# Low sample columns of the normed x moved behind its high columns, in an fp32r decoder step on one core

## The reference

```
h = rmsnorm(x, norm_g) @ w_in            # 12824 columns: q, k, v, gates and z paths of three branches
o_nsa, o_moba, o_mem = three attentions
branches = (o_b * silu(z_b)) @ w_br_b    # for each of the three
y = x + sum(sigmoid(gate_logits) * branches) @ w_out
```

## Time and profile before

| | us |
|---|---|
| median of 3 runs | 1113.56 (1112.87 to 1113.68) |
| span of the profiled execution, first to last instruction | 1110.9 |
| TensorE busy | 1100.0 |
| VectorE busy | 606.3 |
| ScalarE busy | 419.5 |
| GpSimd busy | 66.8 |

### The profile page before, as it was taken

How to read it: one execution, slowest core, us unless ns; L and a number is a source line. 1 busy time by engine, 2 the same in 40 slices (tenths; PEclk the granted TensorE clock), 3 DMA queues, 4 the chain that set the end, 5 groups by cost and what they waited for, 6 DMA issues and landing times.

```text
span 1110.9 us, 19312 instructions
## 1 busy us (share of the span) xinstructions
PE 1100.0 (99%) x8020; PEld 1077.8 (97%) x8020; DVE 606.3 (55%) x884; ACT 419.5 (38%) x566; POOL 66.8 (6%) x121
## 2 busy tenths in 40 slices
PE   9999999999999999999999999999999999999996
PEld 7998999999999999999999999999999999999996
DVE  6794443536456667664454467455455454454445
ACT  6733322424335444443333344333333333333332
POOL 0014000000000000001100000000000000002220
PEclk9999999999999999999999999999999999999998
DMA  8556685544444232358888744544544444464342
GB/s 297 196 189 201 228 279 189 179 152 152 168 147 173 83 113 110 114 171 295 288 277 306 257 149 171 171 171 171 171 167 153 168 145 144 147 242 146 148 150 95
DMA packets 64081, 202.03 MB, mean 182 GB/s; under 512 B 6647, under 2 KB 35607, under 8 KB 45831
## 3 DMA queue, kind: packets, MB, share of 16 engines
q1 hardware_dynamic: 58888, 185.68, 48.8%
q0 software_dynamic: 2400, 10.89, 2.8%
q10 hardware_dynamic: 2718, 4.41, 1.1%
HBM read 193.61 MB, written 11.53 MB: 185 GB/s over the span
## 4 chain that ended last, share of the span: by engine, by line
PE 99%; DVE 1%; issue 0%; DVEq 0%
PE bank L1327 27%; PE bank L1328 27%; PE bank L1329 27%; PE bank L1679 1%; PE bank L1360 1%; PE bank L1455 1%; PE bank L1450 1%; PE bank L1429 1%; PE bank L1428 1%; PE bank L1427 1%; PE bank L1594 1%; PE bank L1517 0%; PE bank L1452 0%; PE bank L1685 0%; PE bank L1345 0%; PE bank L1454 0%
## 5 line engine op out<-in xcount | busy, mean ns | idle before, releaser
L536 ACT ACTIVATE w_hi<-raw 128x2048 fp32r<-128x2048 f32 x140 | 268.1, 1915 | 572.2 <-PE bank L1329 479.9
L1327 PE MATMUL bank<-h_hi,w_hi 128*128 128x320 f32 x1536 | 479.7, 312 | 0.0
L1329 PE MATMUL bank<-h_hi,w_lo 128*128 128x320 f32 x1536 | 474.6, 309 | 0.0
L1328 PE MATMUL bank<-h_lo,w_hi 128*128 128x320 f32 x1536 | 474.5, 309 | 0.0
L814 DVE TENSOR_TENSOR w_lo<-raw,w_hi 128x2048 fp32r<-128x2048 f32 x140 | 325.2, 2323 | 186.4 <-ACT w_hi L536 186.2
L1327 PEld LDWEIGHTS bank<-h_hi,w_hi 128*128 128x128 f32 x1536 | 288.4, 188 | 3.9 <-issue 3.5
L1328 PEld LDWEIGHTS bank<-h_lo,w_hi 128*128 128x128 f32 x1536 | 288.5, 188 | 0.4
L1329 PEld LDWEIGHTS bank<-h_hi,w_lo 128*128 128x128 f32 x1536 | 288.4, 188 | 0.0
L1328 PE MATMUL bank<-oz_lo,w_hi 128*128 128x320 f32 x256 | 78.9, 308 | 0.0
L1329 PE MATMUL bank<-oz_hi,w_lo 128*128 128x320 f32 x256 | 78.8, 308 | 0.0
L1327 PE MATMUL bank<-oz_hi,w_hi 128*128 128x320 f32 x256 | 78.8, 308 | 0.0
(11 more groups left out here) (347 smaller groups left out, 1127.5 us busy)
## 6 DMA issues: line engine op xcount, KB each, us to landing
raw<-in_stream SPq DMA_DIRECT2D x140, 1024.0 KB, 5.0
cmp_t<-in_cmp_pages SPq DMA_DIRECT2D x32, 128.0 KB, 4.2
kt_moba<-in_moba_k SPq DMA_DIRECT2D x16, 256.0 KB, 3.6
kt_mem<-in_mem_k SPq DMA_DIRECT2D x8, 512.0 KB, 6.3
vs_moba<-in_moba_v SPq DMA_DIRECT2D x16, 256.0 KB
vs_mem<-in_mem_v SPq DMA_DIRECT2D x8, 512.0 KB
out_win_old<-in_cache_win POOLq DMA_DIRECT2D x8, 512.0 KB, 3.7
raw<-in_stream SPq DMA_DIRECT2D x10, 256.0 KB, 9.9
```

The source lines that it names most:

```text
L536: nc.scalar.activation(w_hi[:, u], raw[:, u], ACT.Copy).then_inc(hi_ready[u], 1)
L1327: nc.tensor.matmul(out[:, 0:n], w_hi[:, u, kb, :], hi[:, kb, :], start=(kb == first), stop=False)
L1328: nc.tensor.matmul(out[:, 0:n], w_hi[:, u, kb, :], lo[:, kb, :], start=False, stop=False)
L1329: mm = nc.tensor.matmul(out[:, 0:n], w_lo[:, u, kb, :], hi[:, kb, :], start=False, stop=(kb == last))
```

## The change

The storage of h_hi and h_lo (320 + 320 columns a block) is cut anew: `h_wide` has 384 columns a block, the 320 high ones and behind them the 64 low ones of the samples; `h_low` has the 256 low ones of the prompt. With w_hi, a block multiplies h_wide's 384 columns into columns 0 to 384 of the bank, and h_low's 256 into columns 0 to 256; with w_lo, h_wide's first 320. The low part of the samples so ends up in columns 320 to 384 of the bank, and VectorE adds it: it scales it into a spare of 64 columns, scales the 320, and adds the spare to the last 64. The number of matmuls and the total of moving columns of a block (960) stay.

```
+WIDE = TOK + N_SMP
-        h_hi = fixed("h_hi", [P, KB, TOK], f32r)
-        h_lo = fixed("h_lo", [P, KB, TOK], f32r)
+        h_wide = fixed("h_wide", [P, KB, WIDE], f32r)
+        h_low = fixed("h_low", [P, KB, SEQ], f32r)
+        h_hi = h_wide[:, :, 0:TOK]
...
+            def low_columns(kb):
+                dve.wait_ge(hi_x, kb + 1)
+                for lo, c0, c1 in ((h_low[:, kb, :], 0, SEQ), (h_wide[:, kb, TOK:WIDE], SEQ, TOK)):
+                    ins = nc.vector.scalar_tensor_tensor(lo, x_t[:, kb, c0:c1], gains[:, 0, kb:kb + 1], h_hi[:, kb, c0:c1].bitcast(f32),
+                                                         ALU.mult, ALU.subtract)
+                ins.then_inc(lo_x, 1)
+
+            def scaled_tile(u, j, spare, whole, sample, bk=None, scale=1.0):
+
+                bk = W[u] if bk is None else bk
+                dve.wait_ge(w_free[1 - u], j + 1 + u)
+                dve.wait_ge(mm_done[u], j + 2)
+                nc.vector.scalar_tensor_tensor(spare[:], bk[:, TOK:WIDE], scale, inv[:, SEQ:TOK], ALU.mult, ALU.mult)
+                nc.vector.scalar_tensor_tensor(whole, bk[:, 0:TOK], scale, inv[:], ALU.mult, ALU.mult).then_inc(spare_in[u], 1)
+                dve.wait_ge(spare_in[u], j + 1)
+                return nc.vector.tensor_tensor(sample, sample, spare[:], ALU.add)
+
             def key_tile(n, bk, j):
+                if n:
+                    scaled_tile(n % 2, j, spare_a, kv_t[:, 4 + n, :], kv_t[:, 4 + n, SEQ:TOK], bk).then_inc(w_free[n % 2], 1)
+                    return
...
-            def value_tile(u, j, m, n, scale):
-                dve.wait_ge(mm_done[u], j + 2)
+            def value_tile(u, j, m):
                 dve.wait_ge(v_out[u], m * 16 + 16)
-                nc.vector.tensor_tensor(v_tmp[:, u, 0:n], W[u][:, 0:n], scale[:, 0:n], ALU.mult).then_inc(w_free[u], 1)
+                scaled_tile(u, j, spare_b, v_tmp[:, u, :], v_tmp[:, u, SEQ:TOK]).then_inc(w_free[u], 1)
                 split_lo(u, j + 1)
...
+            def wide_block(out, u, kb, start=0, stop=KB - 1):
+                nc.tensor.matmul(out[:, 0:WIDE], w_hi[:, u, kb, :], h_wide[:, kb, :], start=(kb == start), stop=False, skip_group_check=True)
+                nc.tensor.matmul(out[:, 0:SEQ], w_hi[:, u, kb, :], h_low[:, kb, :], start=False, stop=False, skip_group_check=True)
+                return nc.tensor.matmul(out[:, 0:TOK], w_lo[:, u, kb, :], h_wide[:, kb, 0:TOK], start=False, stop=(kb == stop), skip_group_check=True)
```

More of the change, by code:

```diff
@@ L204, in build @@
         ptb_moba = fixed("ptb_moba", [P, 2, P])
+        o_win = fixed("o_win", [P, 64])
+        spare_a = at("spare_a", [P, N_SMP], f32, q_smp_at + 5120)
+        spare_b = at("spare_b", [P, N_SMP], f32, G_ + 4352)
         raw_a = at("raw_a", [P, KB, P], f32, used_up)
@@ L210, in build @@
         g12 = fixed("g12", [P, 2, 2, TOK])
+        spare_c = fixed("spare_c", [P, N_SMP])
         assert top[0] <= F
@@ L887, in _ @@
                     first_gained(n)
-                low_part(h_lo, x_t, h_hi, 0, *HEAD[n], hi_x, lo_x)
+                for kb in range(*HEAD[n]):
+                    low_columns(kb)
                 second_low(n)
@@ L975, in _, with query_tile @@
             ch.settle()
-            def query_tile(u, j, slot):
-                dve.wait_ge(mm_done[u], j + 2)
-                nc.vector.scalar_tensor_tensor(slot, W[u][:, 0:TOK], SCALE, inv[:], ALU.mult, ALU.mult).then_inc(w_free[u], 1)
+            def query_tile(u, j, idx):
+                scaled_tile(u, j, spare_a, one(q_t, idx), one(q_t, idx, N_SMP, SEQ), scale=SCALE).then_inc(w_free[u], 1)
                 split_lo(u, j + 1)
@@ L1116, in _ @@
             for u in range(2):
-                value_tile(u, J_V + 3, 5, TOK, inv)
+                value_tile(u, J_V + 3, 5)
             for u in range(2):
@@ L1331, in part, with wide_part @@
                     mm.then_inc(mm_done[u], 1)
+            def wide_block(out, u, kb, start=0, stop=KB - 1):
+                nc.tensor.matmul(out[:, 0:WIDE], w_hi[:, u, kb, :], h_wide[:, kb, :], start=(kb == start), stop=False, skip_group_check=True)
+                nc.tensor.matmul(out[:, 0:SEQ], w_hi[:, u, kb, :], h_low[:, kb, :], start=False, stop=False, skip_group_check=True)
+                return nc.tensor.matmul(out[:, 0:TOK], w_lo[:, u, kb, :], h_wide[:, kb, 0:TOK], start=False, stop=(kb == stop), skip_group_check=True)
+            def wide_part(u, j, kbs, out=None, spare=False):
+                if kbs[0] == 0:
+                    pe.wait_ge(lo_ready[u], j + 2)
+                    if not spare:
+                        pe.wait_ge(w_free[u], j + 1)
+                for kb in kbs:
+                    mm = wide_block(W[u] if out is None else out, u, kb)
+                if kbs[-1] == KB - 1:
+                    mm.then_inc(mm_done[u], 1)
             ALL, PART_A, PART_B, PART_C = range(KB), range(0, 5), range(5, 10), range(10, KB)
@@ L1350, in second_tile @@
                     pe.wait_ge(lo_x, kb + 1)
-                    nc.tensor.matmul(W[1][:, 0:TOK], w_hi[:, 1, kb, :], h_hi[:, kb, :], start=(kb == 0), stop=False)
-                    nc.tensor.matmul(W[1][:, 0:TOK], w_hi[:, 1, kb, :], h_lo[:, kb, :], start=False, stop=False)
-                    mm = nc.tensor.matmul(W[1][:, 0:TOK], w_lo[:, 1, kb, :], h_hi[:, kb, :], start=False, stop=(kb == KB - 1))
+                    mm = wide_block(W[1], 1, kb)
                 return mm
@@ L1442, in _ @@
             for k in range(4):
-                part(0, J_PHI + k, h_hi, h_lo, TOK, ALL)
+                wide_part(0, J_PHI + k, ALL)
                 c, m = k // 2, k % 2
@@ L1477, in first_value_pair @@
                         pe.wait_ge(v_lo_rdy, kb // 4 + 1)
-                    nc.tensor.matmul(W[1][:, 0:TOK], w_hi[:, 1, kb, :], h_hi[:, kb, :], start=(kb == 0), stop=False)
-                    nc.tensor.matmul(W[1][:, 0:TOK], w_hi[:, 1, kb, :], h_lo[:, kb, :], start=False, stop=False)
-                    mm = nc.tensor.matmul(W[1][:, 0:TOK], w_lo[:, 1, kb, :], h_hi[:, kb, :], start=False, stop=(kb == KB - 1))
+                    mm = wide_block(W[1], 1, kb)
                 mm.then_inc(mm_done[1], 1)
             def value_pair(k):
-                part(0, k + J_V, h_hi, h_lo, TOK, range(0, 3))
+                wide_part(0, k + J_V, range(0, 3))
                 turn_pair(k - 1)
-                part(0, k + J_V, h_hi, h_lo, TOK, range(3, KB))
-                part(1, k + J_V, h_hi, h_lo, TOK, ALL)
+                wide_part(0, k + J_V, range(3, KB))
+                wide_part(1, k + J_V, ALL)
             def prompt_scores(i):
```

87 lines of the change are left out of this document (43 added, 44 removed).

## The result

The kernel with the change takes 1116.62 us (median of 6 runs, 1115.47 to 1117.5), the kernel before 1113.26 (6 runs, 1112.6 to 1113.68): a ratio of 1.003, with a 95% interval of 1.0019 to 1.0042. It is slower by 0.3%. The prediction was 1106.1 us and faster, with a range of 1095 to 1111, so it was wrong in sign and range. The time is that of its second rival, 1116.3.

A forecast was written before the change was run, and what follows sets the result against it. TensorE, busy 99% of the span, was taken to bound the kernel. Matmul gain -10.6, key-tile stalls +2.5 and head +0.6 made -7.5 us, 1103.4 on the span, plus 2.7 kept for the runs' median: 1106.1 us, range 1095 to 1111.

The forecast's parts named there:

- The step that failed: In each block, the second matmul, cut from 320 to 256 columns, falls from 146.7 to 113.3 ns.
- The gain of 10.6 us: TensorE's saving on all products with x: 1584 blocks at 6.7 ns each.
- 384 columns: First matmul of a block: 173.3 ns forecast, bounded by 166.7 below and 180.0 above.
- Rival 1: In each block, 384 columns pay only 256's surcharge, 6.7 ns: gain 21.1 us, time 1096.0; chance 0.26.
- for each begun 256 columns: Rule for TensorE's matmul surcharge: 6.7 ns per begun 256 columns, so 320, 384 and 512 pay two.
- Rival 2: In the blocks TensorE gains nothing, 384 columns taking 180.0 ns; VectorE's 2.7 us loss remains: 1116.3 us; chance 0.14.
- VectorE's debts: Losses from VectorE's extra work at key tiles and head: 2.5 and 0.6 us; 2.7 together in rival 2.
- The first w_lo: Behind four key tiles, w_lo of tile (0, 3) ends at 54.75 us and stalls TensorE 0.96 us.
- The second w_lo: Behind four more key tiles, w_lo ends at 82.61 us and stalls TensorE 1.55 us.
- The head: At the start, x's low columns take two VectorE instructions a block: 0.6 us lost, between 0.3 and 1.5.
- The cover: For nearly all 99 tiles, VectorE's idle time before w_lo hides the extra 0.38 us; without it, 38 us.
- Rival 3: Extra 64-column work also delays TensorE at value transposes or head groups: up to 2 us, 1108; within the forecast's 0.52.

The follow-up runs named there:

- low_moved: The changed kernel with h_low 64 bytes further on in SBUF, slopes and st placed around it: 1107.62 us against 1113.36 for the kernel before.
- streams: TensorE alone, no kernel computed: eleven rows of 96 matmuls by length; 256 columns took 360.0 ns a block, 340.0 begun 448 bytes later.
- tensor_only: The changed kernel without VectorE's extra work on a tile, spare columns left out: 1113.98 us against 1113.24 for the kernel before, ratio 1.0007.
- vector_only: The changed kernel with the old 320 + 320 + 320 shapes but all of VectorE's new work: 1116.37 us against 1113.24 for the kernel before.
- places: TensorE alone, twenty-one rows with x, weights or both begun some bytes further on; mixed block 440.0 ns, 433.3 with h_low 64 bytes on.

## Why the prediction was wrong, step by step

**The step that failed** is "The 256 one falls from 146.7 to 113.3 ns by the earlier trace rows, minus 33.4." shows 256 columns of m_hi and m_lo, and I took the price for one of the length. It hangs on more than the length, the place in SBUF among it: at h_low's place the whole block pays 3 x 13.3 ns beyond its column time, 440.0, as the three 320-column ones did. The gain of 10.6 us on 1584 blocks was 0. With h_low 64 bytes on the block is 433.3 and the gain is there (low_moved against the changed kernel: 9.0 us; 1584 x 6.7 = 10.6, less the blocks that stay above 434 and 0.3 us of longer stalls).

**384 columns** were forecast at 173.3, and cost 173.3 in a row of their own and 173 in low_moved; in the changed kernel 176, with 117 behind it. The sum of a block is what is fixed there, not the parts. Rival 1's block (426.7) was seen nowhere. The reading of the earlier trace rows as one 6.7 ns "for each begun 256 columns" was a rule fitted to four points that differed in place as well as in length, and the rows of streams refute it: begun at a multiple of 128 bytes, 256 and 512 columns pay the same.

**Rival 2** gave the right time, 1116.3 against 1116.6, and the right consequence, nothing gained on TensorE. Its reasons don't hold as written: 384 columns don't take 180, and 256 columns aren't cheap for being in a row of equals (120.0 in such a row in streams) nor dear for standing between longer ones (113 in low_moved). What should have raised its chance above 0.14 was in the rows: the one cheap length in the earlier trace rows was also the only one that read that buffer at that place, so length and buffer could not be told apart there.

**VectorE's debts** came as worked out. A tile's scaling followed by another: 0.91 us for 0.88. The first w_lo ended at 53.11 + 2.28 = 55.39, not 54.75, but 0.54 us of that is the head's delay, which had reached inv (48.48 became 49.02 for the same instruction) and TensorE alike; the stall was 1.04 for a forecast of 0.96 (0.78 in rival 2's version). The second w_lo ended at 80.65 + 2.29 = 82.94, not 82.61, and the stall added 2.59 - 1.56 = 1.03 for 1.55. That forecast had TensorE come earlier by the gain of 59 blocks; without it, as in rival 2, it was 1.33. The head cost 0.45 for 0.6. Together 2.6 to 2.7 for rival 2's 2.7, and tensor_only and vector_only put them on VectorE's extra work separately (0.7 and 3.1 us over their runs of the kernel before; the 0.7 is within its interval of nothing).

**The cover** held elsewhere. VectorE's idle time before w_lo fell from 186.4 us to 140.9, 45.5 us for 99 tiles, 0.46 each instead of 0.38, and no matmul was later for it after 88 us. Rival 3 did not show: the value transposes are within the 0.14 us that were added after 88 us, and the head stayed under its 0.6.

**What stays open** is what sets the price. Many block prices lie 6.7 ns apart (433.3, 440.0; 520.0, 526.7), which is 16 cycles at the granted 2.4 GHz, but not all do (436.7, 443.3, 357.3). They moved with where x starts, and with where the weights do (256 columns in the kernel places: 340.0 a block with either 64 bytes on, 357.3 with both). But the very same bytes gave 433.3 in one program of rows and 443.3 in the next, and 340.0 and 353.3 for the memory keys, and prices of rows failed to come true in a kernel (320 columns with both moved; and oz, whose x lies 64 bytes past a multiple of 128, takes 440 ns a block in every kernel where its row took 436.7). Candidates are the rhythm in which a row begins, the PSUM bank and the place of the instructions; none was tested by itself. So a place has to be tried in the kernel itself.

## What to carry to other kernels

Before a price is taken from a row for another instruction, list everything in which the two differ, the buffer's place included; if the cheap rows all read one buffer, the length isn't shown to be the reason. In a kernel that TensorE bounds, moving an operand by 64 bytes is a cheap thing to try: one such move was worth 9 us here, nearly three times what the change itself moved, and another nothing. The first place of h_low hid a gain that the change had made possible. Work added to VectorE was paid for here only where it was already behind and something urgent was queued after it, and there an addition that nobody needs soon goes behind the urgent instruction.

## What the runs showed of the hardware

A matmul of fp32r columns with a weight load each took its columns plus 13.3 ns at 256, 288, 320, 384 and 512 columns in one layout (16.0 at 448). 256 columns with x begun 32, 64, 96 and 128 bytes on took 118.9, 113.3, 121.1 and 118.3 ns; with nothing moved they took 120.0, or 119.1 with w_lo 128 bytes further on. The 192 columns, at 111.7 ns, took hardly less than 256 at their cheapest. A row that stands twice in one program repeated, but the same operands at the same bytes also had two prices, 113.3 and 117.8 ns a matmul for the memory keys. x of zeros cost the same as x of data.
